# Two TensorE orders in the second block's opening: 16-column products woven between 64-wide ones, and one bias chunk moved ahead of the latent norm's sums

## What is computed

```
h = rmsnorm(x, pre_norm_mix) * (1 + scale_m) + shift_m
proj = h @ w_in        # q_lat 256, kv_lat 128, k_idx 64, w_idx 16, then z, xbc, dt, gates
qn = rmsnorm(q_lat, q_norm);  kv = rmsnorm(kv_lat, kv_norm);  k_idx = rmsnorm(k_idx, kidx_norm)
q = qn @ w_uq;  q_idx = qn @ w_qidx
logits = q @ kv_sel * scale + rel_bias[t5_bucket(pos_sel - pos_q)]   # 16 heads, top-k keys
```

## Time and profile before

| | |
|---|---|
| median of 3 runs | 1496.03 us (1492.23, 1496.03, 1497.35) |
| the profiled execution | 1512.22 us, its span 1510.3 us |
| TensorE busy in it | 1450.2 us, 96% |
| mean granted TensorE clock | 0.974 |

### The profile page before, as it was taken

How to read it: one execution, slowest core, us unless ns; L and a number is a source line. 1 busy time by engine, 2 the same in 40 slices (tenths; PEclk the granted TensorE clock), 3 DMA queues, 4 the chain that set the end, 5 groups by cost and what they waited for, 6 DMA issues and landing times. The chain is left out here.

```text
span 1510.3 us, 22798 instructions
## 1 busy us (share of the span) xinstructions
PE 1450.2 (96%) x9765; PEld 1309.8 (87%) x9765; DVE 932.9 (62%) x1551; ACT 339.4 (22%) x714; POOL 107.6 (7%) x100
## 2 busy tenths in 40 slices
PE   5998999999998999999999998999999999899997
PEld 4866699999876599999989887888888999899986
DVE  3456588574285478768430397741898756766653
ACT  3135112100215222200343213433221201300010
POOL 3000011030000012021000000001000200010120
PEclk8999999999999999999986999999999999999999
DMA  9431357666331177667210531125233444255441
GB/s 307 147 112 57 133 209 275 221 224 223 120 128 60 57 251 251 224 217 267 97 56 0 167 112 56 60 73 178 98 112 112 167 150 153 89 168 168 168 169 55
DMA packets 125012, 222.47 MB, mean 147 GB/s; under 512 B 6105, under 2 KB 33009, under 8 KB 124657
## 3 DMA queue, kind: packets, MB, share of 16 engines
q1 hardware_dynamic: 123418, 218.33, 41.8%
q0 software_dynamic: 1184, 2.56, 0.5%
q10 hardware_dynamic: 311, 0.13, 0.0%
HBM read 218.91 MB, written 2.10 MB: 146 GB/s over the span
## 5 line engine op out<-in xcount | busy, mean ns | idle before, releaser
L1645 PE MATMUL acc<-y,ring 128*128 128x256 f32 (+2 forms) x1360 | 255.2, 344 | 3.2 <-ACT y L782 2.4
L1645 PEld LDWEIGHTS acc<-y,ring 128*128 128x128 f32 (+1 forms) x1360 | 218.9, 192 | 29.4 <-issue 5.0
L1645 PE MATMUL acc<-x,ring 128*128 128x128 f32 (+1 forms) x960 | 160.2, 324 | 0.0
L1645 PEld LDWEIGHTS acc<-x,ring 128*128 128x128 f32 x960 | 144.6, 191 | 12.3 <-issue 1.0
L1645 PE MATMUL acc<-ring,big 128*128 128x256 f32 (+1 forms) x280 | 92.3, 479 | 0.0
L1645 PE MATMUL acc<-hid,ring 128*128 128x128 f32 x736 | 89.6, 276 | 1.3 <-DVE hid L1544 1.3
L1645 PE MATMUL acc<-ysq,ring 128*128 128x128 f32 (+1 forms) x592 | 86.3, 301 | 2.3 <-issue 2.3
L1645 PEld LDWEIGHTS acc<-hid,ring 128*128 128x128 f32 x736 | 85.6, 192 | 1.6 <-DVE hid L1544 1.5
L1645 PEld LDWEIGHTS acc<-ysq,ring 128*128 128x128 f32 x592 | 79.5, 194 | 6.4 <-issue 2.7
L1645 PEld LDWEIGHTS acc<-ring,big 128*128 128x128 f32 x280 | 52.5, 190 | 30.8 <-issue 26.9
L1050 DVE SCALAR_TENSOR_TENSOR ring<-ring,silc 128x512 f32<-128x512 f32 x84 | 70.3, 837 | 3.0
(11 more groups left out here) (417 smaller groups left out, 2616.7 us busy)
## 6 DMA issues: line engine op xcount, KB each, us to landing
ring<-in_w_in SPq DMA_DIRECT2D x24, 2048.0 KB, 8.6
ring<-in_w_up SPq DMA_DIRECT2D x16, 2048.0 KB, 7.9
ring<-in_w_down SPq DMA_DIRECT2D x16, 2048.0 KB, 8.0
ring<-in_ada_w SPq DMA_DIRECT2D x12, 2048.0 KB, 13.3
ring<-in_w_ffn_in SPq DMA_DIRECT2D x22, 1024.0 KB, 6.6
ring<-in_w_out SPq DMA_DIRECT2D x6, 2048.0 KB, 7.9
ring<-in_w_o_ssd SPq DMA_DIRECT2D x4, 2048.0 KB, 7.8
ring<-in_w_ffn_out SPq DMA_DIRECT2D x4, 2048.0 KB, 7.8
```

The lines of the kernel that those rows point to most:

```text
L1645: ins = pe.matmul(dst, w, m, start=start, stop=stop, skip_group_check=True)
```

## The change

On TensorE the 16 products of 16 columns are no longer a stream of their own. One is issued behind each of the 16 products of `k_idx`, into a bank of its own that is taken early. `bias_products(3)` is issued ahead of the latent norm's sums instead of behind them. ScalarE reads the banks in the new order, and the count for which VectorE waits before it overwrites the steps of chunk 3 goes from 13 to 11. No product is added or removed.

```
-BIAS_END = (2, 4, 6, 13, 15, 17, 19, 21)
+BIAS_END = (2, 4, 6, 11, 15, 17, 19, 21)
...
             copied(widx[:, :, :], b[:, :, 0:16], scale=16 ** -0.5 * 64 ** -0.5)
+            bias_back(EARLY_BIAS)
             for i in range(2):
...
-            for ci in range(EARLY_BIAS, 8):
+            for ci in range(EARLY_BIAS + 1, 8):
                 bias_back(ci)
...
-            b = free_bank()
+            b, gates = free_bank(), free_bank()
             for k in range(DC):
                 mm(b[:, 0, :], w[:, k, 256:384], y[:, k, :], k == 0, k == DC - 1)
             for half in range(2):
                 for k in range(DC):
                     ins = mm(b[64 * half:64 * half + 64, 1, :], w[:, k, 384:448], y[:, k, :], k == 0, k == DC - 1)
-            ins.then_inc(filled, 1)
-            b = free_bank()
-            for t in range(TT):
-                for k in range(DC):
-                    ins = mm(b[:, t, 0:16], y[:, k, t * P:(t + 1) * P], w[:, k, 448:464], k == 0, k == DC - 1)
+                    if half == 1 and k == DC - 1:
+                        ins.then_inc(filled, 1)
+                    ins = mm(gates[:, half, 0:16], y[:, k, half * P:(half + 1) * P], w[:, k, 448:464], k == 0, k == DC - 1)
             ins.then_inc(filled, 1)
             to_release[0] += 1
+            bias_products(EARLY_BIAS)
 
             pe.wait_ge(lat_sq, 1)
...
-            for ci in range(EARLY_BIAS, 8):
+            for ci in range(EARLY_BIAS + 1, 8):
                 bias_products(ci)
```

## The result

The changed kernel takes 1503.14 us, the median of 7 runs (1499.46 to 1505.9), against 1496.03 us for 7 of before (1492.23 to 1498.03). The ratio is 1.0035, interval 1.0022 to 1.0049: slower, by 5.2 us on 1496 (the ratio is not that of the medians, which are 7.1 us apart). I had forecast 1483 us, a gain; the time lies above the range, which ended at 1501.

A forecast was written before the change was run, and what follows sets the result against it. TensorE, busy 96% of the span, was taken to bound the kernel through what it issues and its clock. 18.0 us of clock gain less 4.7 of weaving, 13.3, off 1496.03 gave 1483 us; range 1475 to 1501.

The forecast's parts named there:

- the sum carries over: Step from profile to timed runs: the 13.3 us gain is taken from the 1496.03 us median, giving 1482.7.
- the same slow stretch: TensorE's clock at 0.50 from 782.4 to 818.6 in the profile of before, assumed present in the timed runs.
- The clock term: Bias chunks, mean squares, transposes and start of `w_uq` at full instead of half clock: 18.0 us gained.
- Rival 4: Timed runs never had the slow stretch, so only the weave's 4.7 us loss is left: 1501 us; chance 0.08.
- The price of the stretch: Cost of the low clock from the mean squares to the start of `w_uq`: 18.0 us.
- The weave: `k_idx` and 16-column products in pairs: 0.91 us each, 14.5 us where 9.84 stood, a loss of 4.7 us.
- my 0.655 us "apart": Two `k_idx` and two 16-column instructions when not woven: 2 x 0.215 + 2 x 0.1125 us, against 0.91 woven.
- Rival 1: In the weave, weight loads go ahead in spite of changing shapes: gain 18.0 + 0.2, 1478 us; chance 0.13.
- The moved chunk: Bias chunk 3 ahead of the mean squares: covers the wait for the second latent square; nothing waits, no cost.
- a slack: VectorE's steps of chunk 6 ready at 795.5, wanted by TensorE at 797.1: 1.6 us, formerly over 10.
- Rivals 2 and 3: Clock falls part-way through bias chunks, 1490 us, chance 0.13; or no later than before, 1501 to 1506 us, chance 0.12.

The follow-up runs named there:

- e1: The kernel before, unchanged, run again with a new profile: 1497.49 us, ratio 0.9996 to the other executions of before.
- e7: Kernel before with four narrow products woven behind every four `k_idx` products, chunk 3 left in its place: 1497.68 us, ratio 0.9991.
- e10: Kernel before with the 16 narrow products woven behind the 8 `kv_lat` products, two behind each, no chunk moved: 1497.36 us, ratio 0.9998.
- e8: Kernel before with its 16-column stream issued twice: 1507.22 us, ratio 1.0074.
- e11: Repeat of e3, bias chunk 3 moved ahead without the weave, against the kernel before: 1500.36 us, ratio 1.0015.
- e3: Kernel before with bias chunk 3 ahead of the latent norm's sums, the 16-column products left as their own stream: 1500.02 us, ratio 1.0012.

## Why the prediction was wrong, step by step

**The step that failed** is the one that carried the sum over: "the sum carries over if the timed runs hold the same slow stretch". They did not. The clock term of 18.0 us was worked out for a stretch that 4 of 116 executions have. Rival 4 named this, with its price, 1501 us, and I gave it 0.08, because the stretch "would have to be missing in all of" three runs. That was the wrong way round: three runs within 5.1 us of one another, all nearly 15 us or more under the profiled one, say that the profiled one is odd. The sign hung on this alone: without the clock term the sum is a loss of 4.7 us, and the runs showed a loss of 5.2 and of 3.1.

**The price of the stretch** was about right for the execution in which it stands: 57.65 - 40.57 = 17.1 us between the first profile of before and e1, for 18.0 predicted. In time, the three long executions (median 1512.3) lie 14.2 us above the median of 1498.2 of the other 105.

**The weave**: 0.91 us a pair and 4.7 us in all predicted; 0.90 and 4.49 measured. The size was right, the account of it was not whole. I put all of it on the changes of shape, but sixteen pairs at my 0.655 us "apart" are 10.5 us, and the old order took 9.84. I did not ask why: it holds the overlap at the seam of `k_idx`. By e7 3.7 us are the changes of shape and 0.8 the lost overlap; e10, which has neither, loses nothing, so the narrow products by themselves cost no more when woven. The Trainium skill's sentence that a change of tiling mode drains TensorE ("TensorEngine Tiling (Array Packing)", section "Key Properties") agrees with the 0.38 us of idle loads at each return. Rival 1 falls.

**The moved chunk** I put at nothing. Within the change that holds: it runs at 1.00, the mean squares behind it take 1.78 us, and the second latent square is covered. VectorE made the steps of chunks 6 and 7 in 4.49 us from 797.80 on, so those of chunk 6 were ready near 800.1 and wanted at 801.62, a slack of 1.5 us for the 1.6 predicted. Alone it costs 2.2 us (0.7 to 3.9), probably by a fall of the clock that I had not weighed; both profiles have it, but that the move brings it about is not shown.

**Rivals 2 and 3** fall for every execution that left a trace: the changed kernel's two profiles show 1.00 from the weaving to `w_uq`. The page "TensorE: Matmul & The Clock Gate" of the Trainium skill, section "Why this matters for your kernels", names idle gaps of TensorE as what brings the clock down. The prediction says that the trace shows none before 781, which is true of the rows that it shows and not of the whole:

```profile
751.93 3.72 PE L1645 MATMUL ptb<-ysq,ones 128*128 128x256 f32 x16 [1.40 <-ACT ysq L789]
```

This gap of 1.40 us stands 29 us ahead of the fall, and e1 has it too, without a fall. In e8 the clock fell with TensorE busy for 4.70 of 4.70 us, and in e11 for 2.30 of 2.30. These falls have no such gap beside them, so what the page names does not explain them.

**What is left over.** The first ratio is 5.2 us (3.3 to 7.3), the second 3.1 (1.2 to 5.1); the weave's 4.49 us lies in both intervals. The profiles differ by short low stretches elsewhere, such as a clock of 0.50 for a few us near 88, 126 or 755 us in some and not in others. I do not attribute the rest. What decides in which execution the long stretch comes was not found; the same page of the Trainium skill says, in section "What's actually happening", that the monitor behind the clock runs freely and isn't reset when a kernel starts, which would fit, but no run here shows it.

## What to carry to other kernels

Before a cost is read from a profile, ask whether the timed runs had it: here the profiled execution stood 1.1% above the median, and that was the warning, not an overhead. Don't weave products whose weights have another width: each change of shape and back cost 0.245 us here, while the same weave between weights of one width was free. And two 64-wide products into different column halves belong next to one another: also where one run of them ends and the other begins.

## What the runs showed of the hardware that I had not expected

- Two 64-wide products into different halves of PSUM's partitions overlap when they are issued in turn: 16 products in 3.61 us instead of 6.24. Even one half after the other, they overlap where the halves meet, which is worth 0.8 us.
- The same program with the same timeline of TensorE from 759.25 to 779.98 us had the clock fall in one execution and not in another; the difference is 17.1 us by `w_uq`, and it came in 4 of 116.
- The clock falls with TensorE busy without a pause, inside a stream of 16-column products (e8, e11) or 0.5 and 1.1 us behind it (e3, the first profile of before). How long it stays down differs: 10 and 14 us with the mean squares behind one bias chunk (e3, e11), 37 us with five chunks in one piece (before).
